# Layer 1 of a two-layer decoder: the first two blocks of attention scores moved ahead of the last gate job

## The chip, the cores and the metric

One core of one Trainium2 chip runs the whole program. The metric is the device time of one execution in microseconds; lower is better. Engines are named as in the profile: PE is the tensor engine (matmuls), PEld its weight loads, DVE the vector engine, ACT the scalar engine, POOL the GpSimd engine, SP the queue that issues the DMA transfers. Each engine runs its own list of instructions strictly in the order in which it was written; semaphores order the engines among each other.

## The reference, cut to what matters

Two layers over 1024 tokens of width 1024. Layer 0 is latent attention, layer 1 sparse attention with 8 heads in 2 key/value groups. An indexer gives every query a score for every earlier key, and only the 256 best keys of a query take part:

```python
score = einsum('bqhk,bqh->bqk', relu(logits), wi * IDX_HEADS ** -0.5)
_, idx = lax.top_k(score, top_k)                 # 256 keys for each query
s = einsum('bqgrd,bqkgd->bqgrk', qb, k_sel) * HEAD_DIM ** -0.5
pr = softmax(where(valid, s, -inf))
o = einsum('bqgrk,bqkgd->bqgrd', pr, v_sel)
y = (o * jax.nn.silu(z)) @ w_out                 # z: the gate path
```

The kernel does not gather. It finds each query's 256th largest score by a search over the bits of the threshold, turns the scores into a mask of 0 and 1 (ties are resolved by a running count), and attends densely with the mask added.

## The kernel before, in words

`plan()` writes one list of steps; every engine goes through the same list and takes out its own part of each step, so the order of the list is the order of work on every engine. Operands of products are held as a high and a low half (`act_hi`, `act_lo` and so on), and a product is three matmuls (lines 1700 to 1702); so whatever PE is to multiply must first have been split, the high half on ACT (line 1170) and the low half on DVE (line 1341). PSUM has eight banks: ring A (banks 0 to 3) takes projections and scores, the latter two banks at a time, ring B (4 to 7) takes transposes and the products with the values. A step may use a bank only when the step that had it before has been read out.

The part of the program around the change, in layer 1:

- **The gate jobs.** `z_chunk` is called twice and emits 16 projection jobs z0 to z15, each 24 matmuls of 512 columns. ACT applies Silu to each result (line 1254, into a half of the row buffer `p0`), SP stores it to DRAM (line 1032). Jobs 8 to 15 use the weights in ring buffer 1; jobs 12 to 15 read the second half of the tokens in every tile of `act`.
- **The search.** With each gate job goes a step of the search, after job 7 the closing steps: `last_step` with job 8, `above` with job 9, then `sel` for the query blocks 2 to 7 with jobs 10 to 15. A `sel` is four DVE instructions (lines 1638 to 1641: equality, a running sum, a comparison, the final selection) that turn the scores of one block, (t+1)*128 keys wide, into 0 and 1; they use `gz` and `cs` as scratch. Blocks 0 and 1 need no selection.
- **Queries, keys, values of the first head.** The queries are loaded and transposed with job 10 (`q_prep`, PE line 1751, then ACT and DVE). After job 15 come the transposes of key group 0 (`split4` from `p1`), and `v_split`, which splits the values of group 0 (ACT line 1326, DVE line 1692). SP then loads the gate rows of head 0 (line 1047, which waits for all gate stores) and the queries of head 1 (line 1076).
- **The attention loop.** For each head the query blocks come in the order 6, 7, 0, 1, 4, 5, 2, 3. A block goes through S (scores on PE; DVE adds the mask, writes the row and finds its minimum, line 1668), E (Exp on ACT, line 1308; reciprocal and scaling on POOL, lines 1140 and 1141), T (transposes on PE, line 1912; high half on ACT, low half on DVE) and, two blocks at a time, PV (the product with the values on PE, the product with the gate rows on DVE, line 1681). T of a block stands in the list two blocks behind its S. The rows lie in turn in `p1`, `cs` and `p0`.
- **Masks.** In the first head the masks are made on DVE from the selected scores (lines 1653 to 1656) into ring buffer 1, whose last reader is gate job 15. Those of blocks 6, 7 and 0 stand ahead of S of block 6, each further one a block or two ahead of its use; the first waits for job 15, for all `sel` steps and for the last gate stores.
- In the fourth place of each head (`i == 3`) stands `q_prep` for the next head. With head 0 it follows T of block 7.

Of the kernel before, what the change touches and what calls it, by code (L numbers as in the profile page):

```python
# [19 lines left out]
ALU = mybir.AluOpType  # L20
# [7 lines left out]
P = 128  # L28
# [28 lines left out]
RAW_SLOTS = 3  # L57
WARM = 22
# [46 lines left out]
def plan():  # L105
# [147 lines left out]
    def z_chunk(lay, i, base, prefetch=True, extra=None):  # L253
        for job in range(8):
            if prefetch:
                ahead(next_chunk(lay, i), job)
            slot = job % 2
            if lay == 0:
                proj(lay, i, job, ["zr"], {"zr": 1, "zs": 1, "z_st%d" % slot: 1}, slot=slot, base=base)
            else:  # L260
                proj(lay, i, job, ["zs"], {"zs": 1, "z_st%d" % slot: 1}, slot=slot, base=base)
            if extra:
                extra(8 * (base // CW) + job)
# [148 lines left out]
    def s_step(lay, h, qb, q_ready):  # L412
        n = att["n"]
        att["n"] += 1
        s = add("S", {"a_full": 1, "nb": 1}, ring="A", jobs=1, freed=["nb"], wide=True,
                lay=lay, h=h, qb=qb, ps=n % 3, q_ready=q_ready, pe_ld=pe_at[h] if lay == 0 else 0)
        return dict(lay=lay, ps=n % 3, qb=qb, bank=s.banks[0], nb=s.after["nb"])
# [276 lines left out]
    after_bits += [("sel", {"found": 1}, {"t": t}) for t in range(FULL, T)]  # L694

    def z_extra(k):
        search()
        if k == 10:
            first_q["ready"], rd = q_prep(0, ld)
            first_q["v_ld"] = t2_load("v", 0, rd)  # L700
        if not bits and k >= 8 and after_bits:
            kind, incs, kw = after_bits.pop(0)
            add(kind, incs, **kw)
    ld = t2_load("q", 0, ("b_full", now["b_full"]))
# [9 lines left out]
    k_ready, v_ready = {}, {}  # L714
    for j in range(2):
        k_ready[0] = split4("p1", 0, ("k0_ld", k0.after["k0_ld"]), dest="kT", g=0, j=j).after["lo"]

    def v_prep(g, ld, act_free):
        s = add("v_split", {"hi": 1, "lo": 1}, g=g, ld=ld, act_free=act_free)
        v_ready[g] = s.after["lo"]  # L720
        return ("lo", s.after["lo"])
    rd = v_prep(0, first_q["v_ld"], act_free)


    waiting = []
# [59 lines left out]
def build(nc, x, x_t, in_cols, p, positions, norm_in, w_in0, q_norm, kv_norm, w_uq, w_uk, w_uv, w_out0, w_in1, w_out1,  # L785
# [7 lines left out]
    with ExitStack() as ctx:  # L793
# [109 lines left out]
        def kT1(part, g, c0, n):  # L903
            return act[part][:, 4096 + g * 1024 + c0:4096 + g * 1024 + c0 + n]
        def v1(part, g, c0, n):
            return act[part][:, 6144 + g * 1024 + c0:6144 + g * 1024 + c0 + n]
# [260 lines left out]
        def _(act_e):  # L1167
# [4 lines left out]
            for s in steps:  # L1172
# [150 lines left out]
                elif k == "v_split":  # L1323
                    act_e.wait_ge(sem["t2_ld"], n["ld"])
                    act_e.wait_ge(sem["a_full"], n["act_free"])
                    nc.scalar.activation(v1(0, n["g"], 0, S), t2[:], ACT.Copy).then_inc(sem["hi"], 1)
# [3 lines left out]
        def _(dve):  # L1330
# [39 lines left out]
            for s in steps:  # L1370
# [259 lines left out]
                elif k == "sel":  # L1630
# [4 lines left out]
                    eq, order = gz[:, 0:keys], cs[:, 0:keys]  # L1635
                    if t > FULL:
# [5 lines left out]
                                                   ALU.add).then_inc(sem["found"], 1)  # L1642
                elif k == "mask":

                    t = n["t"]
                    if n["first"]:
                        dve.wait_ge(sem["a_full"], n["a_full"])
                        dve.wait_ge(sem["found"], s.before["found"])
                        dve.wait_ge(sem["z_st0"], s.before["z_st0"])
                        dve.wait_ge(sem["z_st1"], s.before["z_st1"])  # L1650
# [6 lines left out]
                elif k == "S":  # L1657
# [9 lines left out]
                    else:  # L1667
                        nc.vector.tensor_tensor_reduce(rows[ps][:, 0:keys], src, mask_at(n["qb"]).bitcast(F32),
# [21 lines left out]
                elif k == "v_split":  # L1690
                    dve.wait_ge(sem["hi"], s.after["hi"])
                    nc.vector.tensor_tensor(v1(1, n["g"], 0, S), t2[:], v1(0, n["g"], 0, S).bitcast(F32),
                                            ALU.subtract).then_inc(sem["lo"], 1)
# [260 lines left out]
```

## Time and profile before

| | us |
|---|---|
| median of 3 runs (1345.52 to 1347.94) | 1345.65 |
| the profiled execution's own time | 1348.37 |
| its span in the trace | 1346.5 |
| busy: PE, PEld, DVE, ACT, POOL | 1302.9, 1111.5, 803.5, 563.1, 524.6 |

The profile is of one execution. The span runs from the first to the last instruction, and the 1.87 us beside it lie around the program. Matmuls overlap in the pipeline, so the busy time of PE is near the span wherever PE has something to do; what tells is where it had nothing to do. A time in brackets behind an instruction is how long its engine was idle before it, and who released it. PEclk, or the clock in the tables by stretch, is the share of full speed (2.4 GHz) that PE was granted; 0.50 is 1.2 GHz.

### The profile page before, as it was taken

To read this page: it belongs to the slowest core of one execution; us is meant where nothing else is said; L and a number is where in the kernel's file an instruction comes from. 1 tells how busy PE (TensorE), PEld (TensorE's weight loads), DVE (VectorE), ACT (ScalarE), POOL (GpSimd) and SP (SyncE) were. 2 spreads that over 40 slices of the span, in tenths; PEclk is the share of its full clock that TensorE was granted. 3 is DMA by queue.
4 is the path that set the end of the run, shared out by engine and by line. 5 is a ranking of instruction groups with operands and counts; after the bars stand their busy time and mean duration, and the time that the engine had idled before them with its cause. 6 is when DMAs were issued, how large, how long until landed. Compare 5 with 4: busy or idle time off the path is not lost. (4 is left out here: it accounts for less than half of the span.)

```text
span 1346.5 us, 19019 instructions
## 1 busy us (share of the span) xinstructions
PE 1302.9 (97%) x6890; PEld 1111.5 (83%) x6890; DVE 803.5 (60%) x1581; ACT 563.1 (42%) x1134; POOL 524.6 (39%) x721
## 2 busy tenths in 40 slices
PE   9999999999999999999987999999899999999997
PEld 8878888989898888888766788888788988888885
DVE  7624755555556345245577889977977776345233
ACT  8312244554454023123235665564266666023122
POOL 2842034554443744234401132331066564744201
PEclk9999999999999999999998999999999999999999
DMA  6232331121101522133300122342222221521122
GB/s 203 77 106 78 112 116 56 55 71 48 55 32 56 175 87 75 60 96 120 95 0 1 55 87 89 110 140 67 88 72 64 79 63 64 153 95 59 60 65 87
DMA packets 83372, 110.07 MB, mean 82 GB/s; under 512 B 9552, under 2 KB 45648, under 8 KB 83280
## 3 DMA queue, kind: packets, MB, share of 16 engines
q1 hardware_dynamic: 83280, 108.86, 26.0%
q8 instruction: 56, 0.92, 0.3%
q14 instruction: 36, 0.29, 0.1%
HBM read 81.04 MB, written 27.79 MB: 81 GB/s over the span
## 5 line engine op out<-in xcount | busy, mean ns | idle before, releaser
L1700 PE MATMUL psum<-ring_hi,act_lo 128*128 128x512 f32 x816 | 322.4, 395 | 0.7 <-DVE act_lo L1688 0.7
L1702 PE MATMUL psum<-ring_hi,act_hi 128*128 128x512 f32 x816 | 318.9, 391 | 0.0
L1701 PE MATMUL psum<-ring_lo,act_hi 128*128 128x512 f32 x816 | 318.8, 391 | 0.0
L1126 POOL CAST ring_hi<-raw 128x512 fp32r<-128x512 f32 x128 | 81.8, 639 | 322.6 <-DMA raw<-in_dsa_w_in 144.0
L1341 DVE TENSOR_TENSOR act_lo<-psum,act_hi 128x512 fp32r<-128x512 f32 (+3 forms) x276 | 156.0, 594 | 67.2 <-ACT act_hi L1170 40.9
L1129 POOL TENSOR_TENSOR ring_lo<-raw,ring_hi 128x512 fp32r<-128x512 f32 x128 | 180.0, 1406 | 10.4
L1700 PEld LDWEIGHTS psum<-ring_hi,act_lo 128*128 128x128 f32 x816 | 154.1, 189 | 32.8 <-DVE act_lo L1688 1.4
L1702 PEld LDWEIGHTS psum<-ring_hi,act_hi 128*128 128x128 f32 x816 | 153.8, 188 | 32.3
L1701 PEld LDWEIGHTS psum<-ring_lo,act_hi 128*128 128x128 f32 x816 | 154.1, 189 | 31.0
L1170 ACT ACTIVATE act_hi<-psum 128x512 fp32r<-128x512 f32 (+1 forms) x244 | 114.9, 511 | 150.2 <-PE psum L1912 80.5
L1140 POOL TENSOR_TENSOR small<-small 128x1 f32<-128x1 f32 x128 | 70.7, 552 | 228.7 <-ACT p L1308 169.8
L1700 PE MATMUL psum<-act_hi,act_lo 128*128 128x256 f32 (+3 forms) x416 | 126.3, 303 | 0.9 <-DVE act_lo L1341 0.4
L1701 PE MATMUL psum<-act_lo,act_hi 128*128 128x256 f32 (+3 forms) x416 | 123.3, 296 | 0.0
L1702 PE MATMUL psum<-act_hi 128*128 128x256 f32 (+3 forms) x416 | 123.0, 296 | 0.0
L1237 ACT ACTIVATE psum<-xr,bits_u 128x512 f32<-128x512 f32 (+2 forms) x96 | 90.3, 941 | 41.3 <-DVE bits_u L1596 35.2
L1700 PE MATMUL psum<-act_hi,ring_lo 128*128 128x512 f32 x256 | 100.7, 393 | 0.8 <-POOL ring_lo L1129 0.8
L1702 PE MATMUL psum<-act_hi,ring_hi 128*128 128x512 f32 x256 | 99.8, 390 | 0.0
L1701 PE MATMUL psum<-act_lo,ring_hi 128*128 128x512 f32 x256 | 99.6, 389 | 0.0
L1529 DVE TENSOR_TENSOR p<-psum,p 128x512 f32<-128x512 f32 x32 | 22.2, 693 | 111.6 <-PE psum L1702 111.6
L1308 ACT ACTIVATE p<-p,small 128x896 f32<-128x896 f32 (+7 forms) x86 | 67.0, 779 | 47.1 <-DVE small L1665 36.0
L1700 PEld LDWEIGHTS psum<-act_hi,act_lo 128*128 128x128 f32 x416 | 79.3, 191 | 7.2 <-DVE act_lo L1341 4.8
L1580 DVE TENSOR_SCALAR_CACHE_REDUCE gz<-xr,bits_u 128x384 f32<-128x384 f32 (+2 forms) x96 | 80.1, 835 | 3.2
(257 smaller groups left out, 2473.7 us busy)
## 6 DMA issues: line engine op xcount, KB each, us to landing
raw<-in_dsa_w_in SPq DMA_DIRECT2D x48, 256.0 KB, 3.1
gz<-z_scratch SPq DMA_DIRECT2D x16, 512.0 KB, 3.6
raw<-in_ple_w_gate SPq DMA_DIRECT2D x32, 256.0 KB, 3.1
raw<-in_mla_w_in SPq DMA_DIRECT2D x19, 256.0 KB, 2.9
xr<-in_x_t SPq DMA_DIRECT2D x16, 256.0 KB, 6.8
z_scratch<-gz SPq DMA_DIRECT2D x16, 256.0 KB, 2.0
raw<-in_mla_w_out SPq DMA_DIRECT2D x16, 256.0 KB, 3.4
p<-in_x SPq DMA_DIRECT2D x16, 256.0 KB, 3.1
```

The lines of the kernel that those rows point to most:

```text
L1126: last = nc.gpsimd.tensor_copy(dst, src[:, c0:c0 + cols])
L1129: last = nc.gpsimd.tensor_tensor(dst, src[:, c0:c0 + cols], hi.bitcast(F32), ALU.subtract)
L1140: linked(nc.gpsimd.tensor_tensor(one_over, sm[:, n["ps"]:n["ps"] + 1], minus_one, ALU.pow))
L1170: nc.scalar.activation(dst, src, ACT.Copy).then_inc(sem["hi"], 1)
L1237: nc.scalar.activation(bank(6, (t + 1) * P), score_at(t), ACT.Sign, bias=u_cand.bitcast(F32)[:, i:i + 1], scale=-1.0, accum_out=cnt[:, i:i ...
L1308: nc.scalar.activation(rows[ps][:, 0:keys], rows[ps][:, 0:keys], ACT.Exp, bias=nb[:, ps:ps + 1], scale=-1.0, accum_out=sm[:, ps:ps + 1]).t ...
L1341: nc.vector.tensor_tensor(dst, src, hi.bitcast(F32), ALU.subtract).then_inc(sem["lo"], 1)
L1529: nc.vector.tensor_tensor(st, bank(s.banks[0]), st, ALU.mult).then_inc(sem["pp"], 1)
L1580: linked(nc.vector.tensor_scalar(gz[:, 0:(t + 1) * P], score_at(t), cand[:, i:i + 1], 0.0, ALU.is_lt, ALU.add, accum_out=cnt[:, i:i + 1]))
L1700: nc.tensor.matmul(dst, lhs(1), rhs(0), start=start, stop=False)
L1701: nc.tensor.matmul(dst, lhs(0), rhs(1), start=False, stop=False)
L1702: return nc.tensor.matmul(dst, lhs(0), rhs(0), start=False, stop=stop)
```

## The change

It moves work of layer 1 in the list of steps and moves buffers so that this is possible:

- The `sel` steps come in the order 6, 7, 4, 5 with jobs 10 to 13. Those of blocks 2 and 3 come in the attention loop of head 0: 2 behind T of block 6 and E of block 0, 3 behind T of block 7 and E of block 1. They use free columns of `xr` as scratch.
- The transposes of key group 0 come with job 12, `v_split` and the load of head 1's queries with job 13.
- With job 14 come two masks into free columns of `xr` (`mask_first`, blocks 6 and 7), then S and E of blocks 6 and 7.
- Job 15 comes behind them; its result goes to ring B.
- The attention loop begins with block 0. There the wait for the last gate stores is in S of block 0 (`z_done`), whose row lies in `p0`. Masks 0, 1, 4, 5, 2, 3 come one with each block; those of blocks 6 and 7, for the later heads, are made with blocks 2 and 3, so DVE makes ten masks where it made eight.
- Keys and values lie in other columns of `act`, group 0 where jobs 12 to 15 do not read. Of `v_split` the operands are two pieces of 512 columns.

```diff
+LATE_SEL = (2, 3)
@@ z_chunk
-                proj(lay, i, job, ["zs"], {"zs": 1, "z_st%d" % slot: 1}, slot=slot, base=base)
+                proj(lay, i, job, ["zs"], {"zs": 1, "z_st%d" % slot: 1}, slot=slot, base=base,
+                     ring="B" if base and job == 7 else "A")
@@ plan, layer 1
-    after_bits += [("sel", {"found": 1}, {"t": t}) for t in range(FULL, T)]
+    after_bits += [("sel", {"found": 1}, {"t": t}) for t in (6, 7, 4, 5)]
@@ z_extra
+        if k == 12:
+            for j in range(2):
+                k_ready[0] = split4("p1", 0, ("k0_ld", k0.after["k0_ld"]), dest="kT", g=0, j=j).after["lo"]
+        if k == 13:
+            first_q["next"] = t2_load("q", 1, v_prep(0, first_q["v_ld"], now["a_full"]))
         if not bits and k >= 8 and after_bits:
             kind, incs, kw = after_bits.pop(0)
             add(kind, incs, **kw)
+        if k == 14:
+            for qb in order[:2]:
+                add("mask_first", None, t=qb)
+            for qb in order[:2]:
+                ps = att["n"] % 3
+                early.append((0, qb, e_step(s_step(1, 0, qb, max(first_q["ready"], k_ready[0]), first=True)), ps))
@@ behind the gate jobs
-    for j in range(2):
-        k_ready[0] = split4("p1", 0, ("k0_ld", k0.after["k0_ld"]), dest="kT", g=0, j=j).after["lo"]
-    rd = v_prep(0, first_q["v_ld"], act_free)
-    waiting = []
+    ld = first_q["next"]
+    waiting = list(early)
@@ the attention loop
-        if h + 1 < HEADS:
+        if h and h + 1 < HEADS:
             ld = t2_load("q", h + 1, rd)
         for i, qb in enumerate(order):
-            if h == 0:
-                for t in (order[0:3] if i == 0 else order[i + 2:i + 3]):
-                    add("mask", None, t=t, a_full=act_free, first=t == order[0])
-            ps = att["n"] % 3
-            args = s_step(1, h, qb, max(q_at[h], k_ready[h // GROUP]))
+            if h == 0 and i >= 2:
+                for t in (qb, order[i - 6]) if i >= 6 else (qb,):
+                    add("mask", None, t=t, a_full=act_free, first=i == 2)
             pv = bool(ready_pv) and i % 2 == 1
-            if len(waiting) > 1:
-                transposes()
-            waiting.append((h, qb, e_step(args), ps))
+            if h or i >= 2:
+                ps = att["n"] % 3
+                args = s_step(1, h, qb, max(q_at[h], k_ready[h // GROUP]), z_done=h == 0 and i == 2)
+                if len(waiting) > 1:
+                    transposes()
+                waiting.append((h, qb, e_step(args), ps))
+            if h == 0 and i in (2, 3):
+                add("sel", {"found": 1}, t=i)
@@ DVE, mask
                     if n["first"]:
                         dve.wait_ge(sem["a_full"], n["a_full"])
-                        dve.wait_ge(sem["z_st0"], s.before["z_st0"])
-                        dve.wait_ge(sem["z_st1"], s.before["z_st1"])
@@ DVE, S of layer 1
+                        if n["z_done"]:
+                            dve.wait_ge(sem["z_st0"], s.before["z_st0"])
+                            dve.wait_ge(sem["z_st1"], s.before["z_st1"])
+                        mask = mask_first(n["qb"]) if n["first"] else mask_at(n["qb"]).bitcast(F32)
```

## Rows read from the trace of the kernel before

**Rows 1.** The page: busy time, share of the span and instructions of each engine.
```profile
PE 1302.9 (97%) x6890; PEld 1111.5 (83%) x6890; DVE 803.5 (60%) x1581; ACT 563.1 (42%) x1134; POOL 524.6 (39%) x721
```
**Rows 2.** Busy time by stretch: length, PE, PEld, DVE, ACT, POOL, PEclk, DMA.
```profile
940.00:967.00 27.00, 27.00 (x120) 22.30 (x120) 26.12 (x30) 3.12 (x6) 0.00 (x0) 1.00 0.21 69
967.00:977.00 10.00, 4.53 (x26) 3.37 (x23) 8.91 (x17) 6.17 (x9) 1.76 (x3) 0.91 0.48 158
977.00:988.00 11.00, 11.00 (x68) 10.74 (x69) 7.92 (x18) 6.63 (x16) 6.97 (x11) 0.77 0.17 49
988.00:1009.00 21.00, 20.14 (x153) 18.65 (x152) 15.86 (x38) 13.67 (x32) 13.05 (x20) 1.00 0.29 89
```
**Rows 3.** Timeline of PE: start, us, instruction [idle before, releaser].
```profile
967.07 1.03 PE L1751 MATMUL psum<-ident,p 128*128 128x128 f32 x8
970.15 0.50 PE L1700 MATMUL psum<-act_hi,kpe_lo 128*128 128x512 f32 x1 [2.04 <-DVE act_lo L1341]
...
974.03 0.30 PE L1700 MATMUL psum<-act_hi,kpe_lo 128*128 128x128 f32 x1 [0.99 <-DVE small L1668]
...
976.99 1.75 PE L1912 MATMUL psum<-ident,p 128*128 128x128 f32 x7 [2.43 <-POOL p L1141]
...
984.66 0.36 PE L1700 MATMUL psum<-act_hi,act_lo 128*128 128x256 f32 x1
...
999.82 1.09 PE L1912 MATMUL psum<-ident,p 128*128 128x128 f32 x8 [0.45 <-POOL p L1141]
```
**Rows 4.** PE alone by stretch: length, busy, PEclk, DMA.
```profile
975.00:976.00 1.00, 0.00 (x0) 0.64 0.69 235
...
982.00:983.00 1.00, 1.00 (x7) 0.95 0.00 0
```
**Rows 5.** Timeline of DVE from the selection steps to head 1.
```profile
943.40 0.41 DVE L1638 TENSOR_SCALAR gz<-xr,bits_u 128x384 f32<-128x384 f32 x1
...
949.50 0.55 DVE L1638 TENSOR_SCALAR gz<-xr,bits_u 128x640 f32<-128x640 f32 x1
...
971.14 0.62 DVE L1656 TENSOR_SCALAR ring_hi<-xr 128x896 fp32r<-128x896 f32 x1
...
972.53 0.23 DVE L1654 CAST ring_hi<-tri 128x128 fp32r<-128x128 f32 x1
972.79 1.09 DVE L1668 CUSTOM_DVE_ANT_0 p<-psum,ring_hi 128x896 f32<-128x896 f32 x1
...
978.77 1.16 DVE L1341 TENSOR_TENSOR act_lo<-psum,act_hi 128x512 fp32r<-128x512 f32 x2 [2.65 <-ACT act_hi L1170]
...
993.71 1.08 DVE L1668 CUSTOM_DVE_ANT_0 p<-psum,ring_hi 128x896 f32<-128x896 f32 x1
...
995.39 1.23 DVE L1668 CUSTOM_DVE_ANT_0 p<-psum,ring_lo 128x1024 f32<-128x1024 f32 x1
```
**Rows 6.** Timeline of ACT: the gates' Silu, the loads of its tables, the first Exp.
```profile
884.78 1.28 ACT L1254 ACT_TABLE_LOAD   x1 [2.50 <-issue]
886.08 0.60 ACT L1254 ACTIVATE p<-psum 128x512 f32<-128x512 f32 x1
...
967.27 0.60 ACT L1254 ACTIVATE p<-psum 128x512 f32<-128x512 f32 x1 [4.85 <-PE psum L1702]
...
968.72 1.07 ACT L1326 ACTIVATE act_hi<-t 128x1024 fp32r<-128x1024 f32 x1
969.80 1.28 ACT L1308 ACT_TABLE_LOAD   x1
973.92 1.04 ACT L1308 ACTIVATE p<-p,small 128x896 f32<-128x896 f32 x1 [2.83 <-DVE small L1668]
```
**Rows 7.** Timeline of SP: the load of the gate rows, behind the last gate store.
```profile
970.19 0.32 SPq L1047 DMA_DIRECT2D gz<-z_scratch  x1
```
**Rows 8.** The gate stores: from their issue to landing.
```profile
DMA to landing us min/median/max: 2.0/2.0/5.4
```
**Rows 9.** Busy time between the first score reductions of heads 0 and 1, as rows 2.
```profile
972.79:993.71 20.92, 17.09 (x110) 15.78 (x109) 15.88 (x38) 12.91 (x30) 11.43 (x17) 0.84 0.33 101
```

More of the change, by code:

```diff
@@ L410, in plan, with s_step @@
     order = [6, 7, 0, 1, 4, 5, 2, 3]
-    def s_step(lay, h, qb, q_ready):
+    def s_step(lay, h, qb, q_ready, first=False, z_done=False):
         n = att["n"]
@@ L415, in s_step @@
         s = add("S", {"a_full": 1, "nb": 1}, ring="A", jobs=1, freed=["nb"], wide=True,
-                lay=lay, h=h, qb=qb, ps=n % 3, q_ready=q_ready, pe_ld=pe_at[h] if lay == 0 else 0)
+                lay=lay, h=h, qb=qb, ps=n % 3, first=first, z_done=z_done, q_ready=q_ready, pe_ld=pe_at[h] if lay == 0 else 0)
         return dict(lay=lay, ps=n % 3, qb=qb, bank=s.banks[0], nb=s.after["nb"])
@@ L693, in plan, with v_prep @@
     after_bits = [("last_step", None, {}), ("above", None, {})]
-    after_bits += [("sel", {"found": 1}, {"t": t}) for t in range(FULL, T)]
+    after_bits += [("sel", {"found": 1}, {"t": t}) for t in (6, 7, 4, 5)]
+    k_ready, v_ready, early = {}, {}, []
+    def v_prep(g, ld, act_free):
+        s = add("v_split", {"hi": 1, "lo": 1}, g=g, ld=ld, act_free=act_free)
+        v_ready[g] = s.after["lo"]
+        return ("lo", s.after["lo"])
     def z_extra(k):
@@ L713, in plan @@
     act_free = now["a_full"]
-    k_ready, v_ready = {}, {}
-    for j in range(2):
-        k_ready[0] = split4("p1", 0, ("k0_ld", k0.after["k0_ld"]), dest="kT", g=0, j=j).after["lo"]
[L718 to L721, printed above, removed]
-    rd = v_prep(0, first_q["v_ld"], act_free)
-    waiting = []
+    ld = first_q["next"]
+    waiting = list(early)
     ready_pv = []
@@ L903, in kT1, with v1_all, mask_first, sel_scratch @@
         def kT1(part, g, c0, n):
-            return act[part][:, 4096 + g * 1024 + c0:4096 + g * 1024 + c0 + n]
+            at = (4 + c0 // CW) * S + g * CW + c0 % CW
+            return act[part][:, at:at + n]
         def v1(part, g, c0, n):
-            return act[part][:, 6144 + g * 1024 + c0:6144 + g * 1024 + c0 + n]
+            at = (6 + c0 // CW) * S + g * CW + c0 % CW
+            return act[part][:, at:at + n]
+        def v1_all(part, g):
+            return act[part][:, 6 * S:8 * S].rearrange("p (a b) -> p a b", b=S)[:, :, g * CW:(g + 1) * CW]
+        def mask_first(t):
+            return xr[:, 36 * P:36 * P + 7 * P] if t == 6 else xr[:, 43 * P:51 * P]
+        def sel_scratch(t):
+            keys = (t + 1) * P
+            if t in LATE_SEL:
+                return xr[:, 36 * P:36 * P + keys], xr[:, 57 * P:57 * P + keys]
+            return gz[:, 0:keys], cs[:, 0:keys]
         def qT1(part, slot, c0, n):
@@ L1325, in _ @@
                     act_e.wait_ge(sem["a_full"], n["act_free"])
-                    nc.scalar.activation(v1(0, n["g"], 0, S), t2[:], ACT.Copy).then_inc(sem["hi"], 1)
+                    nc.scalar.activation(v1_all(0, n["g"]), t2[:].rearrange("p (a b) -> p a b", b=CW),
+                                         ACT.Copy).then_inc(sem["hi"], 1)
         @block.vector
@@ L1634, in _ @@
                     thr = u_cand.bitcast(F32)[:, i:i + 1]
-                    eq, order = gz[:, 0:keys], cs[:, 0:keys]
-                    if t > FULL:
+                    eq, order = sel_scratch(t)
+                    if s.before["found"]:
                         dve.wait_ge(sem["found"], s.before["found"])
@@ L1642, in _ @@
                                                    ALU.add).then_inc(sem["found"], 1)
+                elif k == "mask_first":
+                    t = n["t"]
+                    dve.wait_ge(sem["found"], s.before["found"])
+                    linked(nc.vector.tensor_scalar(mask_first(t), score_at(t), -1.0, -NEG, ALU.add, ALU.mult))
                 elif k == "mask":
                     t = n["t"]
+                    dve.wait_ge(sem["found"], s.before["found"])
                     if n["first"]:
                         dve.wait_ge(sem["a_full"], n["a_full"])
-                        dve.wait_ge(sem["found"], s.before["found"])
-                        dve.wait_ge(sem["z_st0"], s.before["z_st0"])
-                        dve.wait_ge(sem["z_st1"], s.before["z_st1"])
                     if t < FULL:
@@ L1667, in _ @@
                     else:
-                        nc.vector.tensor_tensor_reduce(rows[ps][:, 0:keys], src, mask_at(n["qb"]).bitcast(F32),
+                        if n["z_done"]:
+                            dve.wait_ge(sem["z_st0"], s.before["z_st0"])
+                            dve.wait_ge(sem["z_st1"], s.before["z_st1"])
+                        mask = mask_first(n["qb"]) if n["first"] else mask_at(n["qb"]).bitcast(F32)
+                        nc.vector.tensor_tensor_reduce(rows[ps][:, 0:keys], src, mask,
                                                        -DSA_SCALE, 3.4e38, ALU.add, ALU.min,
@@ L1691, in _ @@
                     dve.wait_ge(sem["hi"], s.after["hi"])
-                    nc.vector.tensor_tensor(v1(1, n["g"], 0, S), t2[:], v1(0, n["g"], 0, S).bitcast(F32),
-                                            ALU.subtract).then_inc(sem["lo"], 1)
+                    nc.vector.tensor_tensor(v1_all(1, n["g"]), t2[:].rearrange("p (a b) -> p a b", b=CW),
+                                            v1_all(0, n["g"]).bitcast(F32), ALU.subtract).then_inc(sem["lo"], 1)
         @block.tensor
```

## The prediction

> **What bounds the kernel now.** I read first the page's busy shares: PE is busy 97% of the span [rows 1], so only a stretch in which PE stands still can give time back, and a vector engine at 60% bounds something only where its work is bunched. The busy time by stretch shows such a place [rows 2]. Up to 967 PE and DVE are both full (27.00 and 26.12 of 27). From 967 to 977 PE is busy 4.53 of 10.00 us and DVE 8.91. From 977 to 988 PE is full, but at a clock of 0.77. From 988 on it runs at full clock with under 5% idle. So the transition from the gate jobs to the attention is the only place that this change can reach.
>
> The timeline of PE gives the pieces [rows 3]. Gate job z15 ends at 967.07, the transposes of the keys follow, and then PE waits 2.04 us for their low half, which DVE delivers only after its last selection; 0.99 us for the first score reduction; and 2.43 us for the scaled row of block 6. Together 5.46 us. The clock follows: it falls to half in the slice 975 to 976 and is back in the slice 982 to 983 [rows 4], some 6.7 us at 1.2 GHz, of which PE worked from 976.99 on. That is 5 us of work at half speed, about 2.5 us lost. 5.46 + 2.5 = 8.0 us is all that the place holds.
>
> What ends the waits is DVE. Its timeline runs without a gap through the selections and masks to the first reduction at 972.79 [rows 5]. So two questions decide: how much earlier does DVE get there, and how much later does it come out at the other end.
>
> **The change, part by part.**
>
> *Ahead of the first scores.* DVE loses the selections of blocks 2 and 3 there, 949.50 - 943.40 = 6.10 us, and the mask of block 0, 0.26 us (972.53 to 972.79) [rows 5]. The first reduction starts at 972.79 - 6.36 = 966.43. Its inputs are there: the key transposes stand behind job 12, 16 us earlier, and DVE gets to their low half between two selections. The second reduction follows, 1.09 and about 1.23 us [rows 5], so DVE is through at 968.75.
>
> *PE.* The transposes (1.03 us) move ahead of z13 and S of blocks 6 and 7 (970.15 to 974.03 - 0.99, 2.89 us [rows 3]) ahead of z15: the same work in another order. Job z15 ends at 967.07 + 1.03 + 2.89 = 971.0. The row of block 6 is ready for its transposes 976.99 - 972.79 = 4.20 us after its reduction, at 970.6, now covered by z15; that of block 7 about 1.5 us later. So PE comes out of the transposes of block 7 at some 973.2, with nearly no idle time: all 5.46 us and the clock's loss are gained up to here.
>
> *ACT.* This is where the order costs. Exp of blocks 6 and 7 stands between the Silu of z14 and that of z15, and Exp and Silu need different tables: the first Silu and the first Exp each have a load of 1.28 us ahead [rows 6]. The change adds two loads. The load for Exp runs while ACT waits for the first reduction (in the trace it starts at 969.80, long before the Exp at 973.92): free as long as that wait lasts. The load back to Silu stands in the path. Exp starts 973.92 - 972.79 = 1.13 us behind the reduction, at 967.56; two of them with their sums take 1.3 us each (1.04 and the read-out, my estimate), to 970.2; the load to 971.5; then the Silu of z15, which could have begun at 971.0. In the trace SP passed its wait for the gate stores 970.19 - 967.27 = 2.92 us after the last Silu began [rows 6, 7]. So the stores are all landed at 971.5 + 2.9 = 974.4. The bounds: a landing took 2.0 to 5.4 us [rows 8], so up to 3.4 us more, and nothing less than this; I take the median, since the store of z15 met it before and the load of queries is out of its way now. In the trace the activation behind a load starts 0.02 us after its end, and a load 0.01 us after the activation ahead of it [rows 6]. The 2.50 us of idle ahead of the load at 884.78 are the far bound: 1.2 us more than the load itself on top of it.
>
> The Trainium skill (ScalarE: Activation LUTs, What ACT_TABLE_LOAD costs) says that each switch costs about 1.38 us of draining beside the 1.28 us load. By that rule the last store would land 1.4 us later than my sum has it. The load at 969.80, directly behind another activation, shows no such gap.
>
> *DVE behind 968.75.* It waits for z15 (the first mask in ring buffer 1), 2.2 us, makes the mask of block 0 (0.26), and then stands at S of block 0 until the gate stores are landed: 974.4 - 971.2 = 3.2 us. Behind this wait are queued the low half of block 6's transposes, the selection of block 2, the mask and reduction of block 1, the low half of block 7, the selection of block 3, the low half of head 1's queries, and everything after; ACT's high half of block 7 stands behind Exp of block 0, which waits for the same reduction. Idle in all 5.4 us.
>
> So count DVE from the first reduction of head 0 to that of head 1. Before: 20.92 us, 15.88 busy, 5.04 idle (2.65 of it one wait for T of block 6) [rows 9, 5]. After: the start is 6.36 earlier, the work is larger by 6.10 + 0.26 + 1.39 (the masks of blocks 6 and 7 a second time, 971.14 to 972.53 [rows 5]), the idle time is 5.4 in place of 5.04. The first reduction of head 1 comes at 993.71 - 6.36 + 7.75 + 0.4 = 995.5: **1.8 us later**. Everything that DVE waited for before (T, the values, the queries) is ahead of it now, so I carry none of the old waits over; up to 0.3 us of new ones at the keys of group 1 may remain.
>
> *What this does to PE.* The first product with values (984.66 before [rows 3]) needs the low half of block 7 and a PSUM bank of ring B; z15 only shifts the ring by one, and the bank is, as before, the one that held the first half of head 1's queries. DVE reads that out at 974.4 + 6.10 (two selections) + 1.16 + 1.3 (low halves) + 1.1 (two reductions, a mask) + 0.6 = 984.7. PE has run through its 7.7 us of lead and stands still on the way there in three waits (head 1's query transposes, T of block 0, this product), about 8 us in all. From here on PE follows DVE: the rows of blocks 4, 5, 2, 3 come late, and at T of block 7 in head 1, which before already waited 0.45 us for a row whose reduction began at 995.39 [rows 3, 5], PE is about 2 us late. Later heads are as before: PE is the bound there, and it does not win lost time back.
>
> *The clock.* Three waits of 2 to 3 us within 12 us are more idle time than the 5.46 that brought the half clock before [rows 3, 4]. It hides in the waits, except for the product at 984.7: 24 matmuls of up to 256 columns, 2.5 us at 2.4 GHz and 5.0 at 1.2. PE had about 1 us of slack there. Bounds 0 (full clock) and +1.3 us; I take 0.9, since half clock lasted some 5 us into the work before.
>
> *At nothing:* the load of head 1's queries goes out about 10 us earlier and isn't waited for in either kernel; the gate rows of head 0 are loaded 4 us later, for a use 14 us on; SP's other entries are covered likewise. `v_split` in two pieces is the same 1024 columns. If that cover were gone, the load would be seen as a wait of DVE at its first product with the gate rows.
>
> Sum: 1.8 + 0.9 = **+2.7 us**. The profiled execution took 1348.37, 1.87 beside its span of 1346.5 and 2.72 above the median; I put the difference on the median: 1345.65 + 2.7 = **1348.4**. The case's own range is +1.8 to +3.4: 1347.4 to 1349.1.
>
> **The rivals.**
>
> 1. *PE keeps its lead* (the other side). Place: the wait for the first product with values. DVE would have to be done with its bank before 982, 2.7 us earlier than before; that is the point from which it decides. For it speaks that 8.0 us are to be had; against it that the releaser is DVE, whose work grows by 1.39 us and whose wait (3.2 us for the stores) is in the same queue. If the gates' Silu went ahead of the Exps or DVE did its selections in less wait than I count, the 8.0 us would come back in part: 3 to 6 us, 1340 to 1342.7. Chance 0.17.
> 2. *The two cancel.* DVE's idle time is nearer 3 than 5.4 (the stores land when SP gets to them, and DVE is let go at the end of z15), and no half clock: 1.8 - 3.2 = -1.4, or up to +1.5 with one half of it. 1344.3 to 1347.2. Chance 0.25.
> 3. *The stores come later still.* A drain at the table switch (+1.2 to +1.4) or a slow landing (up to +3.4), each straight into DVE's wait: 1349.6 to 1351.8. Chance 0.10.
> 4. *The change doesn't do what it says:* S of blocks 6 and 7 would find its bank or keys not ready and hold up z15. The keys' low half is done some 7 us before, and of the banks the latest waits for the Silu of z14, 0.6 us, behind which S of block 6 stands. Chance under 0.03; it would be slower too.
>
> **How the numbers follow.** My case has 0.45, spread over 1347.4 to 1349.1. A measurement of this kernel tells about 0.2%, 2.7 us, from no change: the limits are 1343.0 and 1348.3, and my own point lies on the upper one. Faster: rival 1, 0.17. Same: rival 2 and some 0.15 of my case, 0.40. Slower: the rest, 0.43. The range reaches to the near end of rival 1 and takes in rival 3: 1342.8 to 1351.0.
>
> **What would show it.** Right: no idle of PE above 0.5 us between 960 and 973; two more table loads, the second between Exp of block 7 and the last Silu; a gap of about 3 us on DVE ahead of the third reduction, ended by the stores; three waits of PE for DVE between 973 and 985; the clock at half around 977 to 988; the first reduction of head 1 near 995.5. Wrong: the product with values starting before 982, or DVE idle elsewhere than ahead of the third reduction. A first reduction of head 1 earlier than 993.7 would overturn the forecast.

## The result, and the profile after

The changed kernel takes 1350.54 us (median of 20 runs, 1346.92 to 1352.20), the kernel before 1346.42 in its 20 runs (1344.02 to 1348.63). The ratio is **1.0026, 95% interval 1.0020 to 1.0032**: slower by 3.5 us, or by 4.1 us if the two medians are subtracted, where +2.7 was forecast. The profiled execution took 1351.73 us, its span 1349.9.

The page first, as in [rows 1]:

```profile
PE 1301.4 (96%) x6890; PEld 1109.8 (82%) x6890; DVE 805.6 (60%) x1583; ACT 565.4 (42%) x1136; POOL 525.4 (39%) x721
```

The same matmuls; two more instructions on DVE and two on ACT, the second masks and the table loads. The timeline of ACT [rows 6]:

```profile
928.82 0.60 ACT L1283 ACTIVATE p<-psum 128x512 f32<-128x512 f32 x1 [1.70 <-PE psum L1738]
...
963.27 0.60 ACT L1283 ACTIVATE p<-psum 128x512 f32<-128x512 f32 x1 [3.89 <-PE psum L1738]
963.89 1.28 ACT L1337 ACT_TABLE_LOAD   x1
967.97 1.05 ACT L1337 ACTIVATE p<-p,small 128x896 f32<-128x896 f32 x1 [2.80 <-DVE small L1704]
...
969.11 1.16 ACT L1337 ACTIVATE cs<-cs,small 128x1024 f32<-128x1024 f32 x1
...
970.38 1.28 ACT L1283 ACT_TABLE_LOAD   x1
971.67 0.60 ACT L1283 ACTIVATE p<-psum 128x512 f32<-128x512 f32 x1
```

The first line is the Silu of gate job z8, which in the kernel before began at 928.27. Up to there the two kernels do the same work in the same order, so the changed trace is 0.55 us late before the change has begun; to compare, take 0.55 off every time below. The first table load hides in the wait for the reduction, the second lies bare between Exp of block 7 and the Silu of z15, as forecast.

The timeline of DVE, from the first reduction of head 0 to that of head 1 [rows 5]:

```profile
966.84 1.09 DVE L1704 CUSTOM_DVE_ANT_0 p<-psum,xr 128x896 f32<-128x896 f32 x1
...
971.38 0.23 DVE L1686 CAST ring_hi<-tri 128x128 fp32r<-128x128 f32 x1 [2.30 <-PE psum L1738]
974.92 0.29 DVE L1704 CUSTOM_DVE_ANT_0 p<-psum,ring_hi 128x128 f32<-128x128 f32 x1 [3.32 <-DMA z_scratch<-p]
...
976.21 0.41 DVE L1668 TENSOR_SCALAR xr<-xr,bits_u 128x384 f32<-128x384 f32 x1
...
981.14 0.48 DVE L1668 TENSOR_SCALAR xr<-xr,bits_u 128x512 f32<-128x512 f32 x1
...
984.53 1.28 DVE L1371 TENSOR_TENSOR head_w_lo<-psum,head_w_hi 128x512 fp32r<-128x512 f32 x2
...
989.92 0.42 DVE L1717 TENSOR_TENSOR xr<-psum,gz 128x256 f32<-128x256 f32 x1 [0.84 <-PE psum L1738]
...
993.13 1.29 DVE L1371 TENSOR_TENSOR act_lo<-psum,act_hi 128x512 fp32r<-128x512 f32 x2 [0.46 <-ACT act_hi L1199]
...
997.40 1.08 DVE L1704 CUSTOM_DVE_ANT_0 p<-psum,ring_hi 128x896 f32<-128x896 f32 x1
```

Two waits stand where the forecast put them, for z15 and for the gate stores; behind them the two moved selections (976.21 and 981.14). PE between 973 and 994 [rows 3]:

```profile
975.97 1.09 PE L1787 MATMUL psum<-ident,t 128*128 128x128 f32 x8 [2.23 <-DVE act_lo L1371]
...
980.77 0.30 PE L1948 MATMUL psum<-ident,p 128*128 128x128 f32 x1 [2.73 <-DVE act_lo L1371]
...
985.36 0.36 PE L1736 MATMUL psum<-act_hi,act_lo 128*128 128x256 f32 x1 [2.90 <-DVE head_w_lo L1371]
...
993.97 0.36 PE L1736 MATMUL psum<-act_hi,act_lo 128*128 128x256 f32 x1 [0.50 <-DVE act_lo L1371]
```

PE had no listed wait from 960 to 973.7, where the transposes of block 7 end. Then it stood in three waits, all on DVE, 7.86 us together against 5.46 before. Busy time by stretch, and PE alone where the clock fell (columns as [rows 2, 4]):

```profile
967.00:974.00 7.00, 6.74 (x40) 5.61 (x38) 2.31 (x5) 5.97 (x9) 3.20 (x4) 1.00 0.11 39
974.00:986.00 12.00, 4.40 (x28) 3.77 (x28) 10.74 (x21) 3.64 (x10) 3.84 (x6) 0.99 0.34 110
986.00:998.00 12.00, 11.44 (x67) 9.85 (x66) 10.50 (x25) 6.62 (x16) 5.30 (x8) 0.87 0.22 66
```

```profile
985.00:986.00 1.00, 0.64 (x5) 0.89 0.00 0
986.00:987.00 1.00, 1.00 (x6) 0.50 0.00 0
...
989.00:990.00 1.00, 1.00 (x9) 0.91 0.00 0
```

The place of the loss has moved, not gone: from 967 to 974 DVE now works 2.31 of 7 us while PE is full, and from 974 to 986 DVE is full and PE works 4.40 of 12. By the slices at its edges (0.89 and 0.91) PE was at half clock from 985.8 to 989.2, 3.4 us.

One number sums the stretch up: from the Silu of z8 to the first reduction of head 1. Before 993.71 - 928.27 = 65.44 us, after 997.40 - 928.82 = 68.58, **+3.14**. From there to the end of the span the kernels are alike (352.8 and 352.5 us). The experiments are read by the same number, called the stretch.

### The profile page after: what moved, and what is told of

Same layout as the page of the kernel before. It is cut to its first block and busy times, and to the rows that moved or that the text cites. A ratio compares the mean times of both kernels' runs of the same rounds, so it can differ in the third digit from the quotient of the medians.

```text
span 1349.9 us, 19027 instructions
## 1 busy us (share of the span) xinstructions
PE 1301.4 (96%) x6890; PEld 1109.8 (82%) x6890; DVE 805.6 (60%) x1583; ACT 565.4 (42%) x1136; POOL 525.4 (39%) x721
## 5 line engine op out<-in xcount | busy, mean ns | idle before, releaser
L1158 POOL TENSOR_TENSOR ring_lo<-raw,ring_hi 128x512 fp32r<-128x512 f32 x128 | 180.1, 1407 | 10.4
```

Of the source, the lines that this page charges most:

```text
L1158: last = nc.gpsimd.tensor_tensor(dst, src[:, c0:c0 + cols], hi.bitcast(F32), ALU.subtract)
```

## The experiments

Every experiment was timed beside the kernel before, experiments 1 to 4, 5 to 8, and 9 and 10 each on a chip of their own; so they are compared with each other by their ratio to the kernel before and by the stretch. A stretch comes from one profile. The edits are against the changed kernel unless another is named.

**1. Let S of block 0 wait for the stores of its own half only.** The row of block 0 lies in `p0`'s half that z14 left; z15's half is first written by block 5's row.

```diff
-z_done=h == 0 and i == 2
+z_done={2: 1, 5: 2}.get(i, 0) if h == 0 else 0     # 1: wait z_st0 alone, 2: z_st1 alone
```

> Edit of the changed kernel: S of block 0 writes 128 columns of p0, all in the half of slot 0, so it waits only for the store of z14 (long landed); S of block 5, the next user of p0, waits for that of z15. My theory (the wait for the last gate store holds DVE, and everything queued behind it): the third reduction starts near 971.7 in place of 974.92, DVE then waits about 1 us for the high half of block 6's transposes, and all later DVE work comes 2.2 to 3.3 us earlier: 1347.2 to 1348.4 where the changed kernel has 1350.5. Rival 'late selections' (the two selections in front of the low halves are what PE waits for, whatever starts them): less than 1 us, 1349.5 or more. Rival 'clock' (the half clock is the loss): only as much as the waits shrink enough to keep the clock.

Measured: 1349.54 us beside 1347.26, ratio 1.0016 (1.0007 to 1.0025); stretch 68.10. **A miss** in the time: my theory had 1347.2 to 1348.4. DVE's wait for the stores is gone: the third reduction follows the mask without a gap, 3.2 us earlier than in the changed kernel counted from z8. But head 1 begins only 0.48 us earlier. The timeline of PE and then that of POOL say why:

```profile
976.57 0.30 PE L1949 MATMUL psum<-ident,p 128*128 128x128 f32 x1 [2.43 <-DVE act_lo L1371]
...
982.33 0.69 PE L1949 MATMUL psum<-ident,p 128*128 128x128 f32 x2 [3.85 <-POOL p L1170]
```

```profile
977.57 1.51 POOL L1155 CAST ring_hi<-raw 128x512 fp32r<-128x512 f32 x1 [2.97 <-DMA raw<-in_dsa_w_out]
979.16 1.58 POOL L1158 TENSOR_TENSOR ring_lo<-raw,ring_hi 128x512 fp32r<-128x512 f32 x1
980.71 0.99 POOL L1169 TENSOR_TENSOR small<-small 128x1 f32<-128x1 f32 x1
981.80 0.48 POOL L1170 TENSOR_SCALAR p<-p,small 128x256 f32<-128x256 f32 x1
```

The first piece of the output weights stands in the list ahead of the scaling of row 1. Its load is issued by SP behind the load of the gate rows, and that one waits for the stores. So the stores held up two queues, DVE's and, through SP, POOL's; with the first let go, PE waited 3.85 us for the second. Part of these 3.85 us is POOL itself: the four operations shown take 4.56 us here and 2.96 in the changed kernel. And the clock stood at half from 977.2 to 987.5, 10.2 us against 3.4, so the 2.66 us that are left of the loss are both, waits and clock.

**2. Take the table switch away:** Exp of blocks 6 and 7 behind the Silu of z15.

```diff
@@ k == 14: S of blocks 6 and 7 stay, E is put off
-                early.append((0, qb, e_step(s_step(...)), ps))
+                held.append((qb, s_step(...), ps))
+        if k == 15:
+            for qb, args, ps in held:
+                early.append((0, qb, e_step(args), ps))
```

> Edit of the changed kernel: S of blocks 6 and 7 stays ahead of z15, their Exps go behind the Silu of z15, so that one table load remains of three. My theory: the loads cost only through the last store, which now lands near 974.1 (0.8 us earlier), but the first Exp starts near 973.1 in place of 967.97, T of block 6 near 976.2 in place of 971, and DVE waits for it: slower than the changed kernel by 1 to 3 us, 1351.5 to 1353.5. Rival 'tables' (the two added loads of 1.28 us are the price): faster than the changed kernel by 1.3 to 2.6 us, 1348 to 1349.

Measured: 1353.77 us beside 1347.26, ratio 1.0049 (1.0036 to 1.0062); stretch 71.33. DVE's wait for the stores fell from 3.32 to 2.47 us, so the switch did cost there what a part of a load costs. PE paid for it:

```profile
975.25 1.76 PE L1951 MATMUL psum<-ident,p 128*128 128x128 f32 x7 [4.59 <-POOL p L1173]
```

With the Exps late, the rows of blocks 6 and 7 are late, and all of DVE's queue behind their low halves too (DVE waits 3.55 us at 977.03). The row of block 6 ready early is worth more than the table load that it costs: without both the kernel is 3 us slower. How much of the 3 us is the clock was not separated; it stood at half from 973.1 to 980.0 here, and the seven transposes above took 1.76 us against 0.95. The time is a little above the 1351.5 to 1353.5 that were expected, the direction is the expected one.

**3. Gate job z15 ahead of the first scores** (S and E of blocks 6 and 7 with job 15 in place of 14; their masks stay with 14).

```diff
@@ k == 14: the masks stay; what follows moves
                 add("mask_first", None, t=qb)
+        if k == 15:
             for qb in order[:2]:
                 ps = att["n"] % 3
                 # ... S and E of blocks 6 and 7
```

> Edit of the changed kernel: z15 goes ahead of S of blocks 6 and 7 again, all else stays (selections, transposes, second masks, ring B). My theory: DVE waits for S of block 6 until about 969.5 in place of starting at 966.84, but then finds stores and z15 done: idle 2.9 us in place of 5.6, so it is 2.7 us earlier at head 1: 1347.5 to 1348.5, one table load. A rival that takes the first scores ahead of z15 as what helps (and something else as what costs): slower than the changed kernel.

Measured: 1351.56 us beside 1347.26, ratio 1.0029 (1.0019 to 1.0039); stretch 69.49. **A miss**: 1347.5 to 1348.5 had been expected. The timeline of DVE:

```profile
968.61 1.09 DVE L1705 CUSTOM_DVE_ANT_0 p<-psum,xr 128x896 f32<-128x896 f32 x1 [3.23 <-PE psum L1739]
...
971.31 0.29 DVE L1705 CUSTOM_DVE_ANT_0 p<-psum,ring_hi 128x128 f32<-128x128 f32 x1
...
974.00 1.16 DVE L1372 TENSOR_TENSOR act_lo<-psum,act_hi 128x512 fp32r<-128x512 f32 x2 [2.39 <-ACT act_hi L1200]
```

The waits for z15 and for the stores are both gone, and their 5.62 us are back in two others: 3.23 for the scores, and 2.39 for the transposes of block 6, whose row needs reduction, Exp, scaling and transposes first. I had left out this chain. Moving z15 alone thus takes nothing of the loss away; the stretch is even 0.91 us longer, with the clock at half twice (974.3 to 977.7 and 984.6 to 988.0), while the intervals of the two ratios overlap. DVE has nothing ready to do in these microseconds in either order, because its ready work (the two selections) stands behind the waits.

**4. Keep the clock up:** the score products of blocks 1, 4 and 5 of head 0 are computed 7, 4 and 4 times into the same banks, so that PE works in its waits.

```diff
-                    for c0 in range(0, keys, CW):
+                    again = {1: 7, 4: 4, 5: 4}.get(qb, 1) if lay == 1 and n["h"] == 0 else 1
+                    for c0 in [c for _ in range(again) for c in range(0, keys, CW)]:
```

> Edit of the changed kernel: in head 0 the scores of blocks 1, 4 and 5 are computed 7, 4 and 4 times over into the same bank, 2 to 3 us of matmuls each, which lie in PE's waits. Same result, more work on PE, same waits for DVE. It should keep the clock at full through the first product with values. My theory: the product takes 2.5 us less, of which about 1 us hides: 1349 to 1350, and fewer differences from run to run. Rival 'clock' (the whole loss of 3.5 us is the half clock): 1347. If the repeated scores are themselves in the way, 1351 or more.

Measured: 1349.48 us beside 1347.26, ratio 1.0014 (1.0005 to 1.0024); stretch 67.99. PE alone by stretch:

```profile
973.00:980.00 7.00, 6.53 (x44) 1.00 0.58 187
980.00:990.00 10.00, 9.43 (x67) 1.00 0.00 0
```

Full clock throughout, and 0.59 us of the 3.14 are back. So the clock's share of the loss in the stretch is some 0.6 us by one profile of each; by the ratios it would be 1.6 us, but the two intervals overlap. By either, the waits themselves are the larger part. The time is inside the 1349 to 1350 expected, and far from the 1347 of the rival that put the whole loss on the clock.

**5. Both queues freed:** experiment 1, and the first weight piece loaded and split with job 13.

```diff
@@ k == 13
+            w(chunk_of(1, 7), 0)
@@ attention loop
-            if i == 2:
+            if i == 2 and h:
                 w(chunk_of(1, 7), h)
```

> The half-row wait of e1_half, and the first piece of the output weights is loaded and split with job 13 instead of behind E of block 0. In e1_half POOL stood 2.97 us waiting for that load (SP issued it only behind the load of the gate rows, which waits for all gate stores), then split it, and only then scaled the row of block 1, for which PE waited 3.85 us. My theory (what had moved was the wait for the stores, from DVE to POOL's queue): this gives back 1 to 2 us more, 1347.5 where e1_half has 1349.5 and before 1347.3. Rival 'clock' or 'late selections': POOL's queue doesn't matter, 1349 or more.

Measured: 1348.27 us beside 1347.79, ratio 1.0003 (0.9994 to 1.0012); stretch 65.97. 0.2 us above the kernel before had been expected, and it is 0.4 by the ratio. Freed behind the first, the second queue is worth 2.13 us of stretch, against 0.48 of the first alone; the two together take 2.61 of the 3.14 us away. The clock has a part in it: half for 3.4 us (983.8 to 987.2) where experiment 1 had 10.2. Counted from z8, the product with values starts 1.20 us earlier than there, and the other 0.93 us come behind it. The second queue alone was not tried. PE's waits:

```profile
977.86 0.30 PE L1950 MATMUL psum<-ident,p 128*128 128x128 f32 x1 [2.43 <-DVE act_lo L1372]
...
982.45 0.36 PE L1738 MATMUL psum<-act_hi,act_lo 128*128 128x256 f32 x1 [2.90 <-DVE head_w_lo L1372]
```

**6. The selection of block 2 into DVE's idle time,** ahead of z15, on experiment 5 (with scratch of its own in `xr`).

```diff
@@ k == 14, behind E of block 7
+            add("sel", {"found": 1}, t=2)
@@ attention loop
-            if h == 0 and i in (2, 3):
-                add("sel", {"found": 1}, t=i)
+            if h == 0 and i == 3:
+                add("sel", {"found": 1}, t=3)
```

> e5_w_ahead, and the selection of block 2 goes into the 2.3 us in which DVE waits for z15 (in the list ahead of z15, behind E of block 7). Theory 'DVE's queue is the bound here': its 2.65 us leave the loop and only 0.4 appear ahead: 2 us off, 1345.5 (before 1347.3). Rival (PE's half clock or its own work bounds by now): under 0.7 us.

Measured: 1345.97 us beside 1347.79, ratio 0.9988 (0.9979 to 0.9996); stretch 64.23. PE's waits:

```profile
978.70 0.44 PE L1952 MATMUL psum<-ident,p 128*128 128x128 f32 x2 [0.89 <-POOL p L1173]
...
980.72 0.35 PE L1740 MATMUL psum<-act_hi,act_lo 128*128 128x256 f32 x1 [1.58 <-DVE head_w_lo L1374]
```

Where the kernel of experiment 5 waited 2.43 and 2.90 us, this one waits 0.89 and 1.58, and the stretch is 1.74 us shorter; 2 us had been expected. So the rival 'late selections' of experiment 1 was right in part: the selections in front of the low halves cost as well as the wait for the stores. Here the sign turns: the product with values starts at 980.72, on the right side of the point (before 982) that the prediction named for rival 1.

**7. Less work on DVE:** experiment 6 with the second masks of blocks 6 and 7 made on POOL.

```diff
@@ attention loop, head 0
+                if i == 2:
+                    for t in order[:2]:
+                        add("pool_mask", {"pmask": 1}, t=t, a_full=act_free)
@@ POOL (its two waits left out here)
+                elif k == "pool_mask":
+                    nc.gpsimd.tensor_scalar(mask_at(t), score_at(t), -1.0, -NEG, ALU.add, ALU.mult)
```

> e6_sel2_ahead, and the masks of blocks 6 and 7 for the later heads are made on POOL, ahead of E of block 0, in place of DVE with blocks 2 and 3. DVE has 1.39 us less to do before head 1. Theory 'DVE's queue': up to 1.2 us off, 1344.3 to 1345. If DVE is no longer the bound, or POOL's own row scalings come late for it: 0 or slower by up to 1.

Measured: 1346.20 us beside 1347.79, ratio 0.9991 (0.9983 to 1.0000); stretch 63.80. 1.39 us of work less on DVE brought 0.43 us of stretch and nothing that the times show; up to 1.2 us had been expected from DVE's queue, so this was **a miss**. PE's two waits are 0.21 and 2.90 us, together 3.11 against 2.47 in experiment 6: T of block 1 comes sooner, but the product with values still waits behind the selection of block 3.

**8. The selection of block 3 two blocks later,** on experiment 7: `i == 4` in place of `i == 3`.

> e7_pool_masks, and the selection of block 3 one place later (with block 4, behind the low half of head 1's queries), so that the bank for the first product with values is free 3.3 us earlier while DVE's total stays. If what PE lacks is that bank (and a clock that a shorter wait keeps at full): 1 to 2 us off, 1343 to 1344. If DVE's total work decides: the same as e7 within 0.5.

Measured: 1345.55 us beside 1347.79, ratio 0.9987 (0.9978 to 0.9996); stretch 63.05. The product with values now starts at 977.79, but PE waits further on, 1.34 us for POOL and 1.80 for DVE. The 1343 to 1344 us expected of a bank free earlier did not come; the time is nearer to the other outcome, that of experiment 7 within 0.5 us (0.65 us less, ratios 0.0004 apart).

**9. Experiment 8 with the masks back on DVE.**

> This is e8_sel3_late without its masks on POOL: stores split per half, first weight piece with job 13, selection of block 2 ahead of z15, selection of block 3 with block 4, masks of blocks 6 and 7 again on DVE (1.39 us of it). Theory (DVE's queue order and total work decide, and POOL and DVE slow each other when they work together): moving the 1.39 us back to DVE costs at most 1.4 us in the stretch, less what DVE loses beside POOL (some 0.8 us on the cast and 0.5 us on the mask multiplication seen in e8_sel3_late), so 1345.0 to 1346.5 us, ratio 0.998 to 1.000. Rival (the masks on POOL were what gained): as e8_sel3_late less 1.4 us of gain, 1347 us or above, ratio 1.000 or above.

Measured: 1345.86 us beside 1347.41, ratio 0.9987 (0.9978 to 0.9996); stretch 64.13. As the first theory has it: the masks on POOL are worth 1.08 us of stretch in the profiles, and the two ratios are the same.

**10. Experiment 9 with PE's waits filled** as in experiment 4, blocks 1, 4 and 5 computed 4, 2 and 2 times.

> e9_sel3_dve with the scores of blocks 1, 4 and 5 of head 0 computed 4, 2 and 2 times, so that PE has work in its waits (the results are the same, the work is thrown away). If the clock is what the remaining waits cost, no slice of the stretch stands at half clock and the time falls by 0.5 to 1.5 us against e9_sel3_dve. If the waits themselves cost (DVE late at the values product and at head 1), the time is that of e9_sel3_dve within 0.5 us or up to 1 us more, since the added matmuls (about 2 us) then partly lie in the path.

Measured: 1345.73 us beside 1347.41, ratio 0.9986 (0.9977 to 0.9995); stretch 64.13, to the hundredth that of experiment 9. PE waited in experiment 9, then in this one:

```profile
981.71 0.77 PE L1952 MATMUL psum<-ident,cs 128*128 128x128 f32 x5 [1.38 <-POOL cs L1173]
...
984.27 1.94 PE L1791 MATMUL psum<-ident,t 128*128 128x128 f32 x8 [1.80 <-DVE act_lo L1374]
```

```profile
983.13 1.06 PE L1791 MATMUL psum<-ident,t 128*128 128x128 f32 x8 [1.46 <-DVE act_lo L1374]
...
985.71 0.87 PE L1953 MATMUL psum<-ident,p 128*128 128x128 f32 x6 [0.82 <-POOL p L1173]
```

The half clock of experiment 9 (983.9 to 987.4; eight transposes took 1.94 us against 1.06) is gone, and nothing is gained: PE waits 0.82 us more for POOL instead. In this place the clock costs nothing that the stretch shows. The second of the two expected outcomes came.

The stretch and the ratio side by side:

| kernel | stretch, us | to before | ratio |
|---|---|---|---|
| before | 65.44 | | 1 |
| changed | 68.58 | +3.14 | 1.0026 |
| 1 own half | 68.10 | +2.66 | 1.0016 |
| 2 Exp behind z15 | 71.33 | +5.89 | 1.0049 |
| 3 z15 first | 69.49 | +4.05 | 1.0029 |
| 4 clock kept up | 67.99 | +2.55 | 1.0014 |
| 5 both queues freed | 65.97 | +0.53 | 1.0003 |
| 6 and selection 2 ahead | 64.23 | -1.21 | 0.9988 |
| 7 and masks on POOL | 63.80 | -1.64 | 0.9991 |
| 8 and selection 3 late | 63.05 | -2.39 | 0.9987 |
| 9 as 8, masks on DVE | 64.13 | -1.31 | 0.9987 |
| 10 as 9, clock kept up | 64.13 | -1.31 | 0.9986 |

Among experiments 6 to 10 the stretches lie up to 1.2 us apart and the intervals of the ratios all overlap; these five are not told apart by their times.

## Why the prediction came out as it did

The sign and the mechanism held; the size came out larger than forecast. The measured 1350.54 lies inside the outer range of 1342.8 to 1351.0 but above my own case's 1347.4 to 1349.1, and the +3.5 us by the ratio a little above its +3.4. Of the 2.1 us between it and my 1348.4, 0.8 are the reference, 1346.42 in 20 runs where the forecast started from 1345.65 in three. The upper end of the outer range stood there for rival 3 (a drain or a slow landing), which did not occur; that it took the measurement in was luck. By the prediction's own steps (times of the changed trace less 0.55 where they are compared):

- *Start of the first reduction*, forecast 966.43: 966.84, less the 0.55 us that the trace was late already, 966.29. Right.
- *z15 ends at 971.0, the mask waits 2.2 us:* the wait was 2.30 and ended at 971.38, less 0.55 at 970.83. Right.
- *The table switch lies in the path:* right. Rival 3's drain, which the Trainium skill (ScalarE: Activation LUTs, What ACT_TABLE_LOAD costs) puts at about 1.38 us, did not show: the load began at 970.38, behind the read-out of the last Exp, and the Silu 0.01 us after its end. So this trace does not agree with the page's figure of 2.66 us for a switch; 1.28 is what it measures.
- *Stores landed at 974.4, DVE waits 3.2 us:* SP issued the gate load at 974.84, DVE waited 3.32. Right; the landing took little longer than before, 974.84 - 971.67 = 3.17 us behind the Silu against 2.92.
- *Work on DVE:* forecast 15.88 + 6.10 + 0.26 + 1.39 = 23.63 us between the two first reductions; measured 23.10 of 30.56. Right within 0.5.
- *Idle on DVE*, forecast 5.4: 30.56 - 23.10 = **7.46**. This is the term that was too small. The two named waits make 5.62; the other 1.84 are small gaps and two waits that "up to 0.3 us of new ones" did not hold: 0.84 for the product with values, and 0.46 for block 5's high half. The prediction had carried none of the old waits over, and these two stood in the kernel before too (0.71 and 0.36). The first is also where PE's half clock comes in: at full clock in experiment 4 DVE has no listed wait there. What I had booked as a term beside DVE's chain (0.9) runs back into it. So the sentence "everything that DVE waited for before is ahead of it now" did not hold, and the forecast's own sign of being wrong, DVE idle elsewhere than ahead of the third reduction, showed in this term.
- *Three waits of PE, about 8 us, the product at 984.7:* 7.86 us, and 985.36 less 0.55 = 984.81. Right.
- *The clock, +0.9, half from 977 to 988:* half only from 985.8 to 989.2, worth 0.59 us by experiment 4. The size is inside my bounds, and it fell on the product with values as forecast; the length was wrong. Two waits of 2.23 and 2.73 us passed at full clock, and it fell 0.4 us behind the end of the third. The product's 24 matmuls took 4.36 us against 2.89 before (985.36 to 989.72 and 984.66 to 987.55): 1.5 us more and not 2.5, and at full clock they take 2.9 us, not 2.5.
- *"At nothing":* right for the changed kernel, where DVE's own wait for the stores covered it. But the load of the weight piece, which I called covered, stood behind the same stores through SP and POOL. It cost nothing only while DVE waited longer; experiment 1 took that cover away, and 3.85 us of PE's time stood there. The prediction listed the queue and did not look at whom POOL makes wait.

The total: the reduction of head 1 came at 996.85 on the time of before, 1.35 behind the forecast 995.5. Of this 0.9 was to come later, as the clock's term; 3.14 against 2.7 is what is left of the difference. The step that was mis-sized is thus DVE's idle time, forecast 5.4 and measured 7.46; 0.5 us less work than forecast took a part of it back.

Rivals 2 to 4 did not come: DVE's idle time was 7.46 us and not near 3, the stores landed on time, and S of blocks 6 and 7 found bank and keys ready, since PE has no listed wait there. The first (PE keeps its lead) named the right condition: DVE out of its bank before 982. Experiments 1, 5 and 6 reach it step by step (983.7, 982.5 and 980.5 on the time of before, where the changed kernel has 984.8), and at 6 the kernel is faster than before. What it had too large is the price: it gave 3 to 6 us, and the best of these kernels have 1.6 to 1.9 (ratios 0.9988 to 0.9986). Where the rest of the 8.0 us goes is shown in part: with the first waits gone, later ones open (experiment 9) at T of block 4's row (POOL, 1.38) and at group 1's keys (DVE, 1.80), and DVE's work in the stretch is about what it was. That DVE's total work is the last bound is not shown; experiment 7 took 1.39 us of it off and saw 0.43.

The version of experiment 9 is faster than the kernel before by 0.13% (0.04 to 0.22%), a small gain and the best of several tries, and so faster than the changed kernel. Experiment 10 is no better, and experiment 8 needs more code for the same time.

## What to carry to other kernels

In this kernel, moving work of the bound engine (PE) ahead began to pay only when the engine behind it (DVE) had ready work for the time in which the new order made it wait; put such work ahead of the wait in its queue, not behind. Before a wait for a DMA is placed, list every queue that it reaches, the issuing engine's next loads and their readers among them: here one store held DVE directly and POOL through SP, and the one that the trace of the changed kernel did not show was worth more, freed second, than the one that it did, freed first. And read such a change by the distance between two fixed instructions, not by the span, when parts of the trace that the change doesn't touch vary by a microsecond or two.

## What the runs showed of the hardware that was not expected

- DVE and POOL can slow each other. In experiment 1 POOL's cast took 1.51 us, where the changed kernel has 0.61, and beside its next operation a selection step on DVE took 1.63, where the changed kernel has 0.75. In experiment 8 a DVE cast of 128x128 took 1.03 us beside POOL's scaling, against 0.23 elsewhere; it ended at 973.03, just behind POOL's scaling (971.83 to 972.96). The Trainium skill (SBUF — State Buffer, SBUF: two separate sides) describes such a thing: the two share a pair of ports as an exclusive lock, and the one that comes second is blocked for the other's whole instruction, if the DVE instruction is in a mode that uses two ports, or has two inputs in SBUF while POOL's reads SBUF. The end of that cast agrees with it; whether the cast was in such a mode no view here shows. Not every pair is slowed: a low half that DVE reads from PSUM took its usual 1.28 us beside POOL's L1158 (changed kernel, 979.94). So work moved from DVE to POOL (experiment 7) is not simply taken off DVE. The cast, from DVE's timeline, and the scaling, from POOL's, of experiment 8:

```profile
972.00 1.03 DVE L1696 CAST ring_hi<-tri 128x128 fp32r<-128x128 f32 x1
```

```profile
971.83 1.13 POOL L1180 TENSOR_SCALAR cs<-cs,small 128x1024 f32<-128x1024 f32 x1
```

- The half clock does not follow the sum of the waits. In the changed kernel waits of 2.23 and 2.73 us, 4.96 together, passed at full clock and it fell behind a third of 2.90; in experiment 9 it fell behind 1.38 and within 1.80, 3.18 together; in experiment 10 it did not fall at 1.46 and 0.82. It lasted 3.4 us in the changed kernel and in experiment 9, and 10.2 in experiment 1.
- Spells of half clock come and go in parts of the program that are the same in all kernels: the profiles of the kernel before and of the changed one have such spells near 668, 702 and 719 (the kernel before one more near 730), that of experiment 4 only the one near 669. Its Silu of z8 came at 926.75, that of the changed kernel at 928.82. That this is a good part of the spread from run to run is likely and not shown, since only one run of each kernel has a profile; three of the changed kernel's 20 runs, at 1346.9 to 1347.4 us, show a mean clock of 0.997, the others 0.989 to 0.995 at 1349.4 to 1352.2.
